# Attention on one Trainium2 core: where TensorE transposes the next unit's probabilities, relative to the steps of the sink attention

## The reference, cut to what matters

```python
def swa_gqa_sinks(q, k, v, sinks):                       # branch A, 8 heads on 2 key heads, 128 keys
    scores = einsum(qc, kb) * HEAD_DIM ** -0.5
    m = maximum(max(scores), sink)
    p = exp(scores - m)
    probs = p / (sum(p) + exp(sink - m))
    return einsum(probs, vb)

def chunk_relbias_attention(q, k, v, rel_bias):          # branch B, 8 heads, 9 chunks of 64 keys
    scores = einsum(qc, kb) * HEAD_DIM ** -0.5 + rel_bias[:, idx]
    return einsum(softmax(scores), vb)
```

## Time and profile before

| what | value |
|---|---|
| time, median of 3 runs | 2434.94 us (2433.95 to 2437.76) |
| the profiled execution's own time | 2437.68 us |
| its span, first to last instruction | 2435.8 us |
| mean granted TensorE clock over the span | 0.972 |
| attention | about 781.5 to 1102 us of the span |
| TensorE busy over the span | 94% |

### The profile page before, as it was taken

One profiled execution on the slowest core, in us unless ns is written; L12 is line 12 of the kernel. 1 busy time (PEld: TensorE's weight loads), 2 busy tenths in 40 slices (PEclk: granted clock), 3 DMA queues, 4 the chain that ended last, 5 costly groups with the idle time before them and its releaser, 6 DMA issues. The chain is left out here.

```text
span 2435.8 us, 36728 instructions
## 1 busy us (share of the span) xinstructions
PE 2288.6 (94%) x12226; PEld 1966.1 (81%) x12227; DVE 1300.3 (53%) x1939; ACT 1030.6 (42%) x1817; POOL 815.8 (33%) x782
## 2 busy tenths in 40 slices
PE   7999999999999999998899999499999999999990
PEld 6888887888887988887899998388888888888880
DVE  7112223111010888886333332877767678789885
ACT  6111112111112878874222221456556466667663
POOL 0355455560000111123222221245434434555450
PEclk9999999999999999998999999699999999999995
DMA  5357756641232776755544542699978889899987
GB/s 190 105 155 242 239 195 195 199 166 68 76 126 97 233 233 181 229 133 183 182 149 142 157 129 90 218 307 311 314 232 285 281 257 321 284 367 346 320 286 290
DMA packets 236537, 518.52 MB, mean 213 GB/s; under 512 B 24978, under 2 KB 91682, under 8 KB 235300
## 3 DMA queue, kind: packets, MB, share of 16 engines
q1 hardware_dynamic: 164020, 352.57, 41.5%
q0 software_dynamic: 30048, 86.79, 14.8%
q10 hardware_dynamic: 42384, 78.07, 8.9%
HBM read 385.64 MB, written 131.70 MB: 212 GB/s over the span
## 5 line engine op out<-in xcount | busy, mean ns | idle before, releaser
L468 DVE TENSOR_TENSOR pj_w_lo<-pj_w_raw,pj_w_hi 128x1024 fp32r<-128x1024 f32 x38 | 49.1, 1292 | 524.4 <-ACT pj_w_hi L343 524.4
L343 ACT ACTIVATE pj_w_hi<-pj_w_raw 128x1024 fp32r<-128x1024 f32 x38 | 40.2, 1059 | 532.0 <-PE pj_bank L562 478.0
L2315 POOL TENSOR_TENSOR ex_wd_lo<-weights_raw_d,ex_wd_hi 128x1024 fp32r<-128x1024 f32 x64 | 202.3, 3183 | 122.6 <-ACT ex_wd_hi L2217 118.7
L562 PE MATMUL pj_bank<-pj_hT_lo,pj_w_hi 128*128 128x512 f32 x864 | 230.9, 389 | 0.0
L562 PE MATMUL pj_bank<-pj_hT_hi,pj_w_lo 128*128 128x512 f32 x864 | 230.9, 389 | 0.0
L562 PE MATMUL pj_bank<-pj_hT_hi,pj_w_hi 128*128 128x512 f32 x864 | 230.9, 389 | 0.0
L562 PEld LDWEIGHTS pj_bank<-pj_hT_lo,pj_w_hi 128*128 128x128 f32 x864 | 162.2, 188 | 33.7
L562 PEld LDWEIGHTS pj_bank<-pj_hT_hi,pj_w_hi 128*128 128x128 f32 x864 | 162.2, 188 | 33.7
L562 PEld LDWEIGHTS pj_bank<-pj_hT_hi,pj_w_lo 128*128 128x128 f32 x864 | 162.2, 188 | 33.7
L2419 DVE TENSOR_TENSOR ex_wd_lo<-weights_raw_d,ex_wd_hi 128x1024 fp32r<-128x1024 f32 x64 | 162.5, 2577 | 4.0 <-ACT ex_wd_hi L2217 4.0
L1846 PE MATMUL mg_y_ps<-first_hi,mg_w_hi 128*128 128x256 f32 x512 | 149.1, 291 | 14.4 <-DVE mg_w_lo L1728 6.6
(11 more groups left out here) (333 smaller groups left out, 5826.9 us busy)
## 6 DMA issues: line engine op xcount, KB each, us to landing
weights_raw_g<-in_w_exp_gate_dram SPq DMA_DIRECT2D x128, 512.0 KB, 10.1
weights_raw_u<-in_w_exp_up_dram SPq DMA_DIRECT2D x128, 512.0 KB
weights_raw_d<-in_w_exp_down_dram SPq DMA_DIRECT2D x128, 512.0 KB
pj_w_raw<-in_w_feat_dram SPq DMA_DIRECT2D x38, 512.0 KB
scratch_gates<-pj_f_hi ACTq DMA_DIRECT2D x32, 512.0 KB, 4.9
mg_g_in<-scratch_gates SPq DMA_DIRECT2D x120, 128.0 KB, 2.8
pj_x_in<-in_x_dram SPq DMA_DIRECT2D x16, 512.0 KB, 4.2
scratch_qk<-pj_f_hi ACTq DMA_DIRECT2D x16, 512.0 KB, 7.2
```

The source lines that it names most:

```text
L343: act.activation(w_hi[n % 2][:], w_raw[n % 2][:], ACT.Copy).then_inc(whi_done, 1)
L468: dve.tensor_tensor(w_lo[n % 2][:], w_raw[n % 2][:], w_hi[n % 2][:], ALU.subtract).then_inc(wlo_done, 1)
L562: last = pe.matmul(eight[4 * p + b][:], w[p][:, k * P:(k + 1) * P], h[:, k, b * NB:(b + 1) * NB], start=(k == 0 and n == 0), stop=(k == KD ...
L2315: pool.tensor_tensor(wd_lo[p][:, j, :], raw.buffer[2][j][:], wd_hi[p][:, j, :], ALU.subtract).then_inc(d_lo_pool, 1)
```

## The change

In TensorE's loop `turn_p(0)` is issued ahead of the loop, and iteration u then issues `turn_p(u + 1)` (with `turn_tails` after an odd unit) right behind `scores(u + 3)`, in front of the parts of the sink steps, where before it stood behind them at the head of iteration u+1. Nothing else is changed: not the instructions, their waits, or the loops of the other engines.

```diff
             pe.wait_ge(idt_in, 16)
+            turn_p(0)
             for u in range(LAST + 1):
-                if u < B_UNITS:
-                    turn_p(u)
-                    if u % 2 == 1:
-                        turn_tails(u // 2)
                 if 2 <= u < B_UNITS + 2:
                     (values_shared, values_alone)[u % 2](u // 2 - 1)
                 if u + 3 < B_UNITS:
                     scores(u + 3)
+                if u + 1 < B_UNITS:
+                    turn_p(u + 1)
+                    if u % 2 == 0:
+                        turn_tails(u // 2)
                 if 0 <= u - V_START < V_BATCHES:
                     a_turn_v(u - V_START)
                 s = a_step(u, 5)
                 if s is not None:
                     a_values(s)
                 s = a_step(u, 2)
                 if s is not None:
                     a_turn_p(s)
                 s = a_step(u, 0)
                 if s is not None:
                     a_scores(s)
```

## The result

| | before | changed |
|---|---|---|
| time, median of 7 runs each | 2437.07 us (2433.95 to 2437.84) | 2444.77 us (2443.59 to 2446.49) |
| ratio, with its 95% interval | | 1.0028 [1.0019, 1.0038] |
| profiled execution, its span | 2437.68 us, 2435.8 us | 2443.59 us, 2441.7 us |
| mean granted TensorE clock | 0.972 | 0.974 |

The changed kernel is slower by 0.28%, by the medians 7.7 us. The forecast was +7.2 us. As a time it was 2442.1 us against 2444.77: 2.1 of these 2.7 us come from the median of the kernel before, which was 2434.94 us in the forecast's three runs and is 2437.07 us in seven.

A forecast was written before the change was run, and what follows sets the result against it. TensorE set the pace, busy 287.81 of 303.50 us, its waits being for VectorE; 5.15 + 2.15 - 2.1 + 1.2 + 0.5 + 0.3 = +7.2 us on 2434.94 gave 2442.1 us, range 2433.5 to 2448 (8 in 10).

The forecast's parts named there:

- Term 1: Ten sink turns followed by an iteration without sink part but with `a_collect`: `scores` 0.60 or 0.43 us later, +5.15 us.
- Term 2: Ten sink turns followed by an iteration without sink part, `a_collect` already done: VectorE's lag covers part of the delay, +2.15 us.
- Term 3: Ten sink turns followed by another sink step's scores: the earlier unit turn brings ScalarE in earlier, -2.1 us.
- Term 4: `a_negmax` later on VectorE, reaching `scores` in ten places where the next iteration has no sink part, +1.2 us.
- Term 5: Two single places: `turn_tails` of pair 57 waits for an exponential, +0.5 us; last sink step's scores end later, +0.3 us.
- Rival A: No change: earlier ScalarE and VectorE cancel the sink parts' delay; +0.5 us, 2435.4 us, chance 0.32.
- Rival C: Clearly slower: VectorE becomes the bound, 32 us new idle time, half reaching TensorE, +16 us, 2451 us; chance 0.07.
- Rival B: Faster: TensorE's waits for `maxed` vanish as `pt_main` clears VectorE earlier; -6.5 us, 2428.4 us; chance 0.07.
- The order of the queues: ScalarE and VectorE keep `a_pt` ahead of the ready `pt_main`; were it otherwise, the sum would be -1.3 us.
- the prediction's 0.65 us: Ready `pt_main` held from 924.25 to 924.90 us behind other-branch work, taken as agreeing with strict queue order.

The follow-up runs named there:

- the mirror: Kernel before, TensorE's order unchanged, with `a_pt` moved behind `pt_main` and `pt_tail` on ScalarE and VectorE: 2448.95 us, before 2435.91, ratio 1.0044.
- the partial kernels: Changed kernel with the unit's turn ahead only of sink turn (2445.41 us), only of sink scores (2436.9 us), or only of values without a sink turn (2436.2 us).
- by place: Changed kernel, turn ahead of sink parts only in chosen iterations, `a_pt` behind on ScalarE and VectorE unless the iteration has sink scores: 2433.49 us, ratio 0.9985.

## Why the prediction was right, step by step

**Direction, place and size** held: +7.7 us by the medians against +7.2, all of it idle time of TensorE inside the attention (+7.05 us), with its work and clock unchanged.

**Term 1** (+5.15 us) measured +5.35, the ten places at 0.31 to 0.66 us. (Their waits of before ran from none to 1.18 us, a wider spread than the prediction's 0.31 and 0.45; the sum did not hang on it.) It is the term that was best founded, as both engines were seen idle at the sink turn's end. That the other engines' order makes it, not the sink turn's delay alone, is shown by three kernels: it is gone with `a_pt` behind on both engines, there with ScalarE's alone behind, and back in the mirror.

**Term 2** (+2.15 us) was over-sized. The places themselves are +2.39 us, but the `scores` right in front of them, behind the sink turn, came 1.46 us earlier, so the pair nets +0.93. The prediction said that in Terms 1 and 2 the gain is lost again; then it must also be seen that it is first won. It sized the loss against `scores` before the gain and left the gain out. The kernel ahead of the sink turn alone, which has no gain to give back, loses 1.54 us here: the loss itself was 0.6 us too high, and another 0.6 us is gain that is kept (1.46 us won, 0.85 given back).

**Term 3** (-2.1 us) measured -2.08 us in its ten places, where a sink step's scores follow: -1.85 us in nine of the V T column, with -0.40 us at the place of the earlier trace rows, and -0.23 us in one with no sink values in front, which the table has under rest. The other ten of the V T column are the 1.46 us just named, and make its -3.31 us. The gain comes half from overtaking the scores, half from overtaking the values, as the partial kernels show; the prediction named the scores only.

**Term 4** (+1.2 us) was under-sized, +2.38 us in eleven places of 0 to 0.54 us. The wait of `a_negmax` rose from 2.6 us to 16.2 us and less of it was covered than the 0.15 to 0.5 us of room that I gave each place. That it is this wait is shown by the kernel that moves `a_negmax`, and by the one that overtakes the sink scores alone.

**Term 5**: the early turn of the sums waited, as foreseen, by 0.47 us in its row (0.5):

```profile
1064.61 0.27 PE L1300 MATMUL at_tail_ps<-at_idt,at_sink 128*16 128x128 f32 x1 [0.47 <-ACT at_prob L1034]
...
1099.45 0.69 DVE L1199 TENSOR_REDUCE at_a_top<-at_ax_ps 128x4 f32<-128x512 f32 x1 [3.10 <-PE at_ax_ps L1364]
1100.18 0.17 DVE L1202 SCALAR_TENSOR_TENSOR at_a_neg<-at_a_top,at_nsink 128x4 f32<-128x4 f32 x1
...
1101.74 0.36 PE L1321 MATMUL at_o_ps<-at_pt_hi,at_v_st 128*128 128x256 f32 x1 [1.17 <-DVE at_o_both L1173]
```

At the end, `a_negmax` waits 3.10 us where it waited 1.45, and then its small instruction takes 0.17 us instead of 1.52. From the last `biased` to the end of the stage it is 15.33 us after 14.79, +0.54 us against +0.3.

So Term 2 too high by 1.2 us and Term 4 too low by 1.2 us cancelled. That is luck: the sum is nearer than its parts.

**Signs that did not come as told.** `scores` was to wait 17 us for `maxed` and waits 11.3, since 4.9 us more now stand at `values_shared`. So it is with the places of Term 1, which were to wait 0.9 us each. In the five of even units the wait did rise, by 0.31 to 0.43 us. In the five of odd units `values_shared` stands right in front of `scores`, and the wait there is as before, at most 0.46 us. The last of them shows both waits:

```profile
1072.91 0.39 PE L1321 MATMUL at_o_ps<-at_pt_hi,at_v_st 128*128 128x256 f32 x1 [0.57 <-DVE at_pt_lo L1161]
...
1074.58 0.50 PE L1272 MATMUL at_s_ps<-at_k_st,at_q_st 128*128 128x512 f32 x1 [0.45 <-DVE at_neg L1154]
```

The step that failed is the statement that TensorE waits for nothing but `biased`. It was nearly true of the kernel before, where `values_shared` waited 0.8 us for `pt_main`, but the values of a pair also hang on VectorE's `pt_main`, and the same delay reaches them first. The sum didn't depend on it, as it was counted in the starts of `scores`.

**The rivals.** Rival A (no change) is excluded by the interval and by Term 1. Rival C was nearly right in its idle time: VectorE's waits for the two sink parts rose from 2.6 + 6.5 = 9.1 to 16.2 + 20.8 = 37.0 us, 27.9 us more where it had 32. But of that about a third reaches TensorE, 5.35 + 2.39 + 2.38 = 10.1 us, and 6.8 us are left after the gain of 3.31. Rival B's mechanism does exist, and is seen once the orders match: TensorE's wait for `maxed` falls to 7.6 us, not to 3.

The order of the queues was the hinge. At the place of the earlier trace rows the 0.10 us of before became 1017.49 - 1015.59 = 1.90 us in which `pt_main` stood ready behind `a_pt`, 1.41 us of them with ScalarE idle; the prediction's 0.65 us was another place, with ScalarE busy. The Trainium skill's sentence that the queues of ScalarE, VectorE and GpSimd are strict FIFO (page "PSUM — Partial Sum Buffer", section "Engine vs sequencer instructions") is borne out by that row.

## What to carry to other kernels

When several engines work down hand-written lists and meet at semaphores, moving a step in one list is a change of order for all that wait on both neighbours: give each consumer the same relative order, or expect to pay the overtaking step's duration wherever the consumer has no slack (here 0.31 to 0.66 us in ten places, out of a move that adds no work). A buffer can bind the order as well: here `a_pt`, moved behind, held `ax_ps` longer, and TensorE waited for that where sink scores came early. Size such a move by the interval between the starts of the pacing step, kind by kind of its neighbourhood; the row of waits can stay where it is while the wait moves to another step. And large idle times of the other engines (here 27.9 us more) say little: look for what of them reaches the engine that sets the pace.

## What the runs showed beyond that

`copy_o` waited for an earlier store of its buffer in seven of the eleven experiments' traces, up to 3.41 us with the tails left behind and 2.42 us by place, and in neither the kernel before nor the changed one. It is not a matter of speed alone: the kernel with ScalarE's order alone is slower than before and has it too. All these waits lie in two short stretches, from 874 to 883 and from 1033 to 1043 us. What sets them off no run shows; any further gain here has to deal with them.

The small `a_negmax` instruction on 128x4 elements took 1.52 us in the earlier trace rows and 0.17 us at the same place after the change. It is the only one of the 32 in that trace that took more than 0.17 us. It ended at 1094.27 us and a multiplication on GpSimd at 1094.24; after the change the last multiplication had ended at 1096.84, before the instruction began at 1100.18. That the two share something is what these rows suggest; no run was made to settle it. The Trainium skill has a rule that fits (page "SBUF — State Buffer", section "Terms", the entry on the shared port pair): VectorE and GpSimd take one pair of ports as a lock for a full instruction, and the loser blocks.
